# A hybrid encoder trunk: the forget gate's exponential earlier on ACT, one gate unit split, branch projections in halves

## The reference, cut to what matters

```python
for l in range(DEPTH):                       # 2
    h = rmsnorm(x, g_mix[l])
    fox_p, dsa_p, rwkv_p, gate_p = _split(h @ w_in[l], (FOX_IN, DSA_IN, RWKV_IN, GATE_W))
    o_fox = fox_attention(...)               # 4 heads, forget gate: cumsum(log_sigmoid(f_logit + bias))
    o_dsa = dsa_attention(...)               # index scores, top 64 keys, latent attention
    o_rwkv, v_first = rwkv7_time_mix(...)    # 8 heads of 64, a recurrence over the tokens
    gates = sigmoid(gate_p + b_gate[l]).reshape(B, S, 3, D_MODEL)
    merged = (gates[:, :, 0] * (o_fox @ p_fox[l]) + gates[:, :, 1] * (o_dsa @ p_dsa[l])
              + gates[:, :, 2] * (o_rwkv @ p_rwkv[l]))
    x = x + merged @ w_out[l]
    h2 = rmsnorm(x, g_ffn[l])
    x = x + (swiglu(h2, ...) if l % 2 == 0 else moe_ffn(h2, ...))   # dense, then top 2 of 8 experts
return rmsnorm(x, g_final)
```

## Time and profile before

| | |
|---|---|
| median of 3 runs | 1888.19 us (1883.44 to 1894.51) |
| the profiled execution's own time | 1888.6 us |
| its span in the profile | 1886.9 us |
| mean granted TensorE clock | 0.982 of full speed |
| TensorE busy | 1811.0 us, 96% of the span |
| VectorE busy | 392.7 us, 21% |
| ScalarE busy | 234.1 us, 12% |
| mixers of the first layer | about 25 to 345 us of the span |
| mixers of the second layer | about 581 to 912 us |

### The profile page before, as it was taken

The page is one execution under the profiler, slowest core; times in us unless marked ns, Lnnn a source line. Parts: engine busy times, 40 slices in busy tenths (PEclk is TensorE's granted clock), DMA queues, the critical chain, the costliest instruction groups (busy, mean ns, idle before and its releaser), DMA issues.

```text
span 1886.9 us, 42790 instructions
## 1 busy us (share of the span) xinstructions
PE 1811.0 (96%) x19764; PEld 1165.7 (62%) x19764; DVE 392.7 (21%) x807; ACT 234.1 (12%) x460; POOL 44.6 (2%) x102
## 2 busy tenths in 40 slices
PE   6999999999999999999799999999999999999996
PEld 5787878788887778878535444353443534445344
DVE  1256233100001456133310101101010010101102
ACT  1324120100001324111100000000000000000001
POOL 3000200000000000100000000000000000000000
PEclk9999999999999999989799999999999999999998
DMA  6432212543434332212899999999999999999970
GB/s 189 156 134 90 92 52 84 190 166 133 174 102 140 112 134 90 92 46 90 334 342 375 393 383 401 372 381 389 370 415 370 386 376 378 414 378 383 369 294 24
DMA packets 122842, 462.13 MB, mean 245 GB/s; under 512 B 9567, under 2 KB 20497, under 8 KB 106289
## 3 DMA queue, kind: packets, MB, share of 16 engines
q1 hardware_dynamic: 122672, 459.46, 64.0%
HBM read 458.39 MB, written 1.05 MB: 243 GB/s over the span
## 4 chain that ended last, share of the span: by engine, by line
PE 95%; DVE 2%; ACT 1%; issue 1%; SPq 0%; DMA 0%; DVEq 0%; ACTq 0%
PE bank L1030 31%; PE bank L385 26%; PE bank L1047 15%; PE bank L909 4%; PE bank L869 3%; PE bank L730 2%; PE bank L856 1%; PE bank L984 1%; PE bank L994 1%; PE bank L692 1%; PE bank L424 1%; PE bank L371 1%; PE bank L379 1%; PE bank L783 0%; PE bank L661 0%
## 5 line engine op out<-in xcount | busy, mean ns | idle before, releaser
L1030 PE MATMUL bank<-slot,xg 128*32 128x512 f32 (+1 forms) x6144 | 581.9, 539 | 0.0
L385 PE MATMUL bank<-h,slot 128*128 128x256 f32 x2176 | 488.0, 384 | 8.0 <-ACT rel L1478 5.3
L385 PEld LDWEIGHTS bank<-h,slot 128*128 128x128 f32 x2176 | 415.1, 192 | 70.5 <-issue 14.2
L1030 PEld LDWEIGHTS bank<-slot,xg 128*32 128x32 f32 x6144 | 198.9, 110 | 372.3 <-issue 369.0
L1047 PE MATMUL bank<-slot,aT 128*32 128x256 f32 x5376 | 293.0, 379 | 0.0
L1047 PEld LDWEIGHTS bank<-slot,aT 128*32 128x32 f32 x5376 | 174.9, 110 | 118.6 <-issue 6.2
L2154 DVE TENSOR_TENSOR av<-gs,bank 128x512 f32<-128x512 f32 (+1 forms) x48 | 29.8, 622 | 577.0 <-PE bank L1030 575.0
L909 PE MATMUL bank<-hid,slot 128*128 128x256 f32 x352 | 77.0, 380 | 0.9 <-DVE hid L2022 0.9
L909 PEld LDWEIGHTS bank<-hid,slot 128*128 128x128 f32 x352 | 66.9, 190 | 10.2 <-issue 1.2
L1622 ACT ACTIVATE gs<-bank 128x512 f32<-128x512 f32 (+1 forms) x48 | 25.2, 543 | 284.6 <-PE bank L1030 284.5
L869 PE MATMUL bank<-sq,slot 128*128 128x256 f32 x256 | 56.2, 379 | 0.0
(11 more groups left out here) (407 smaller groups left out, 1086.9 us busy)
## 6 DMA issues: line engine op xcount, KB each, us to landing
slot<-in_moe_w_gate SPq DMA_DIRECT2D x32, 2048.0 KB, 12.5
slot<-in_moe_w_up SPq DMA_DIRECT2D x32, 2048.0 KB, 17.9
slot<-in_moe_w_down SPq DMA_DIRECT2D x32, 2048.0 KB, 10.5
slot<-in_moe_w_gate SPq DMA_DIRECT2D x32, 1536.0 KB, 9.0
slot<-in_moe_w_up SPq DMA_DIRECT2D x32, 1536.0 KB, 11.1
slot<-in_moe_w_down SPq DMA_DIRECT2D x32, 1536.0 KB, 8.8
slot<-in_w_in SPq DMA_DIRECT2D x20, 2048.0 KB, 8.1
slot<-in_ffn_w_gate SPq DMA_DIRECT2D x5, 2048.0 KB, 7.8
```

Of the source, the lines that this page charges most:

```text
L385: ins = mm(o, w[:, k, c:c + n], rhs[:, k, :], start=k == 0, stop=k == nk - 1)
L1030: ins = mm(o.rearrange("s (b c) -> s b c", c=32), xg[:, g, k, :], strip(w[:, kk, :], p), start=k == 0, stop=k == KD - 1)
```

## The change

Three edits, the same in both layers.

1. On ACT, the Exp and the Ln of the forget gate move up in front of the copies of dq and iq, and a Sqrt of one column is added behind them.
2. On TensorE, gate unit 1 leaves its place between the LoRA products and ks. Its first half goes in front of ol, its second half behind do; do's first two heads wait for ol0 alone. ACT's place for the unit stays.
3. The eight branch units are issued in halves: one half before the wait for xl's copies, one behind zl (before the wait for Tf), one in the place of each former unit in the chunks, one behind each Z (before the wait for Zs), three behind Y in the place of the first half of gate unit 10, two behind gm. Gate unit 10's halves each move one place back. VectorE's `weigh` moves accordingly: none in chunk 3, none after Z1, two behind Yz.

```diff
@@ tensor
                 gate_unit(0)
                 probs_t("d")
+                gate_half(1, 0)
                 need_sb(pe, L + "ct")
...
-                need_sb(pe, L + "ol0")
-                need_sb(pe, L + "ol1")
                 b = v2(open_bank(pe, L + "do"))
                 for hh in range(4):
+                    if hh % 2 == 0:
+                        need_sb(pe, f"{l}ol{hh // 2}")
                     p0 = 64 * (hh % 2)
...
                 close_bank(ins, L + "do")
-
+                gate_half(1, 1)
...
-                gate_unit(1)
                 need(pe, "masks", 1)
...
-                def branch(nm, src, off, nk, g, w):
...
-                fill = [("pf", oF, 0, g) for g in range(4)] + [("pd", oD, 2, g) for g in range(4)]
+                fill = [("pf", oF, 0, g, j) for g in range(4) for j in range(2)]
+                fill += [("pd", oD, 2, g, j) for g in range(4) for j in range(2)]
...
                 def filler():
 
-                    nm, src, off, g = fill.pop(0)
-                    if nm == "pd" and g == 0:
+                    nm, src, off, g, j = fill.pop(0)
+                    n = f"{l}{nm}{g}"
+                    if nm == "pd" and g == 0 and j == 0:
                         pe.wait_ge(slot_full[load_at[L + "pa"][0]], 16 * load_at[L + "pa"][1])
-                    branch(nm, src, off, 2, g, wb)
+                    if j == 0:
+                        half["p"] = v2(open_bank(pe, n, 6 + g % 2))
+                    m = 2 * g + j
+                    for k in range(2):
+                        ins = mm(half["p"][:, j, :], wb[:, off + k, m * P:(m + 1) * P], src[:, k, :],
+                                 start=k == 0, stop=k == 1)
+                    if j:
+                        close_bank(ins, n)
                     if not fill:
-                        free_slot(L + "pa", f"{l}pd3")
+                        free_slot(L + "pa", n)
...
                             close_bank(ins, f"{l}zl{q}")
+                filler()
                 need(pe, "t_copied", 6 * (l + 1))
...
                         close_bank(ins, f"{l}Z{c}")
+                        filler()
...
-                gate_half(10, 0)
-
+                for i in range(3):
+                    filler()
                 for nm in ("Y0", "Y1", "Yz0", "Yz1"):
...
                 filler()
+                filler()
                 need(pe, "gsq", 2 * l + 2)
...
-                gate_half(10, 1)
+                gate_half(10, 0)
                 need(pe, "ginv", l + 1)
...
+                gate_half(10, 1)
                 gate_unit(11)
@@ scalar
                 evac(L + "ik", ik[:, :], lambda b: b[:, 0:T])
+                need(act, "fox_z", l + 1)
+                A(ft[:, :], ft[:, :], ACT.Exp, scale=-1.0).then_inc(S["fox_e"], 1)
+                need(act, "fox_e", l + 1)
+                A(ft[:, :], ft[:, :], ACT.Ln, bias=cst[:, 4:5]).then_inc(S["fox_l"], 1)
+                step(A(junk[:, :], cst[:, 4:5], ACT.Sqrt))
                 evac(L + "dq", dq[:, :, :], v2)
...
-                need(act, "fox_z", l + 1)
-                A(ft[:, :], ft[:, :], ACT.Exp, scale=-1.0).then_inc(S["fox_e"], 1)
-                need(act, "fox_e", l + 1)
-                A(ft[:, :], ft[:, :], ACT.Ln, bias=cst[:, 4:5]).then_inc(S["fox_l"], 1)
@@ vector
-                        weigh()
+                        if c < NC - 1:
+                            weigh()
...
                         need_sb(dve, n)
-                        weigh()
+                        if c != 1:
+                            weigh()
...
                     done(tt_(o, o, b, ALU.add), f"{l}Yz{i}")
+                weigh()
+                weigh()
```

## The result

The changed kernel takes 1871.46 us in the median of six runs (1866.33 to 1874.45), the kernel before 1886.33 (1882.97 to 1894.51): a ratio of 0.9917, 95% interval 0.9895 to 0.9939, which is 11 to 20 us or 0.8% faster. The forecast was 1867, in a range of 1859 to 1880. So the direction and the range held, and of the 21 us that I added up some 15 came.

The account below looks back on a forecast made before the run. TensorE, busy 96% of the span, bounds the kernel, so only its idle or low-clock time can be gained. 5.3 + 3.1 + 1.6 + 6.4 + 4.4 = 20.8 us off 1888.6 gives 1867 by the median, range 1859 to 1880.

Parts of the forecast that it names:

- Part 1: Forget gate on ACT: TensorE's wait for rel goes, 5.3 us, and the clock's fall over r0 and r1, 3.1.
- Part 2: Gate unit 1 split over the selected attention: 2.7 us of waits a layer go, new ones come, 1.6 gained.
- ksq's time: First layer, before ks: third sigmoid can start at 155.3, ksq is ready at 159.1, a new wait of 1.7 us.
- Part 3: Branch projections in halves in the scan: waits at Tf and Zs go, 6.4 us for two layers.
- Tf's wait: In the scan: the 0.97 us wait for Tf gets a half unit, 0.9 gained a layer.
- a half is 0.96 (1.99 less its overlap, halved): Length in us taken for each half of a branch unit used as fill in the scan.
- The clock in the scan: Second layer's first scan chunk: the clock's fall to near 1.2 GHz goes with the idle, 4.4 us gained.
- The clock kept no falls at r0 or in the scans: Rival: falls follow small products, not idle, so 3.1 and 4.4 us are not gained: 1875; chance 0.14.
- part 2's waits did not vanish: Rival: ACT's queue is shorter than counted, so part 2 gains 2 x 2.7 instead of 1.6: 1863; chance 0.08.
- VectorE was late at Gs: Rival: behind the gate product in the scan, three chunks a layer by 0.7, 4.2 us less: 1872; chance 0.08.
- the waits did not move to Gs and SA: Rival: waits only move, to Gs and SA and in part 2; part 1's 5.3 and some clock left: 1881; 0.08.
- the clock did not stay low with halves: Rival: clock stays at 1.2 GHz through the scans, 4.4 us a chunk, 31 in all, slower: 1898; chance 0.04.

Follow-up runs that it names:

- e1: The kernel before with the ACT edit alone (forget gate's Exp and Ln moved up, Sqrt added): 1876.49 us, ratio 0.9953.
- e5: The changed kernel with two idle table switches on ACT put in front of rel: 1875.64 us, ratio 0.9947 to the kernel before.
- e2: The kernel before with the split of gate unit 1 alone: 1883.92 us, ratio 0.9988.
- e9: The changed kernel unaltered, run again as a second set of six: 1870.85 us, ratio 0.9927 to the kernel before.

## Why the prediction was right, and where its sizes were off

*Part 1*, 8.4: right in both terms, 5.3 for the wait and 2.8 for the fall where I had 3.1. e1 measured 9 (6 to 12), e5 brought wait and fall back together. The drain of about 1.38 us that the Trainium skill (ScalarE: Activation LUTs, What ACT_TABLE_LOAD costs) puts behind a table load did not show: 1.29 from the start of a load of 1.28 to its activation.

*Part 2*, 1.6: the mechanism is right, waits and places as forecast; e2 measured 2 (0 to 5). In the profile the stretch from dt0's transposes to ks in the first layer is 18.47 where it was 18.88, 0.4 shorter instead of 0.8; to vt in the second layer 28.76 instead of 29.32, 0.6 instead of 0.8. The step that failed by 0.2 to 0.4 is ksq's time: the third sigmoid started 2.0 behind zw's start, not 1.8, since zw's second bank closes later than I had it; and the half between do and zw takes 3.65 from start to start (142.37 to 146.02), where I had counted 3.5. What the prediction did not price is the fall of the clock behind the new wait at vt: 1.7 us between vt and the next stage in the first profile (15.41 ahead of the kernel before at vt, 13.75 ahead at L661); it is missing in e9's profile, where the clock stood at 1.00 behind vt.

*Part 3*, 6.4 without the clock: waits right, size wrong. Tf's wait gave 0.8 for 0.9. From one SA to the next, less the half that moved out, a chunk was shortened by 0.31, 0.88 and 0.77 where I had 0.53, 0.93 and 0.93: mostly the 0.19 for the added return, and the 0.1 at Gs. The whole stretch from L715 to the third branch's projection takes 51.0 in the two scans of whole units without a fall, 48.8 in the first layer of the profile after, and 48.9 in the mean of the twenty with halves: 2.1 a layer, 4.2 for both, not 6.4. The 0.5 a layer between the chunks' sum and this was lost behind the last SA, mostly in a pause of TensorE's sequencer in the products of Y. The failed step is "a half is 0.96 (1.99 less its overlap, halved)".

*The clock in the scan*, 4.4: confirmed as a mean, 4.8 (4.1 in the chunks alone), over six scans with and twenty without whole units. That the sum's one fall came so near the mean is luck: single scans lost 0, 1.6 or 4.5 in their chunks.

With the corrected sizes the sum is 8.1 + 1.0 + 4.2 + 4.8 = 18.1, less up to 1.7 behind vt: 16 to 18, in the upper part of the interval of the first set (11 to 20) and at the end of that of the second (10 to 17). The last 1 to 3 us are not accounted for. Up to 0.7 of it stands where the dense channel mixer begins: before, its first product waits 2.67 for h; after, it waits 3.18 for the load of ffn_w_gate, and 2.7 to 3.4 over the profiles in which it waits for that load. The falls in the levels vary from profile to profile by more.

*The rivals.* The clock kept no falls at r0 or in the scans; part 2's waits did not vanish; VectorE was late at Gs by 0.1 in two chunks a layer, not by 0.7 in three; the waits did not move to Gs and SA; the clock did not stay low with halves.

## What to carry to other kernels

Before moving filling work to a wait, write down what it covered where it stood: here 2.7 us of wait a layer went and 2.1 came back two stages later, and cutting the filler finer, so that it covers both places, won 6 us more, some 3 of them visible in the waits. Count what each cut costs: a fill between small products has a fixed price at its edge, so halving a unit does not halve its time. And count the clock with the wait: the idle of 2.1 to 2.7 in front of r0 cost another 1.4 to 1.7 at the lower clock, in every profile that had it, though waits of 2 elsewhere did so only 3 times in 10.

## What the runs showed of the hardware

A run of full products (128*128 by 128x256, 0.216 us a record) between blocks of small ones takes 0.19 us more than its records, 0.10 where it begins and 0.09 where it ends, for runs of 4, 8 and 16 alike (1.06, 1.92, 3.65). Cutting the block of 32-wide products in two costs a further 0.14 (1.36 for 1.22).

The same instructions can differ by 3.3 us before any edit is reached. This is the chain at the kernel's first norm and first projection, before and after:

```profile
25.34 5.25 PE bank L379 x16
30.59 10.36 PE bank L385 x48
40.95 8.08 PE bank L424 x32
```

```profile
23.59 3.69 PE bank L379 x16
27.29 10.36 PE bank L385 x48
37.65 8.08 PE bank L424 x32
```

The first of them runs partly at 1.2 GHz in one (granted clock 0.70 over its 5.25) and not in the other (1.00 over 3.69). The rest of the difference is older: the products ahead of it (L371) take 6.64 and 5.18. Over all thirteen profiles the projection of L424 begins either at 37.7 to 38.4 or at 40.4 to 41.9. So of the 22.3 us between the two profiles' spans 3.3 had nothing to do with the change, and another 1.5 came the same way at the second layer's first projection. A pair of profiles shows where time went; how much, only several runs do.
